# Two-block transformer kernel on one core: decay products at half width, decay subtractions on POOL, lower bounds computed once, dense groups in another order

## The chip, the core and the metric

The kernel runs on one core of a Trainium2 chip. It is written instruction by instruction: each engine (PE, DVE, ACT, POOL, and SP, which issues the DMAs) has its own list, and the engines meet only at semaphores that the program names. The metric is the device time of one execution in microseconds. Before the change the median of three runs is 3160.41 us (3159.9 to 3169.08).

## The reference, cut to what matters

Two blocks of two layers each work on 512 tokens of width 1024. The change is in the first block alone. Each of its layers projects the normed input and feeds three mixers: an mLSTM, an HGRN2, and a sliding-window attention with sinks. What bears on the change is the HGRN2 and its gate:

```
lb_all = jnp.cumsum(jax.nn.softmax(hgrn_lb_logits, axis=0), axis=0)
lb_all = lb_all - lb_all[0:1]                      # one lower bound per layer and column
...
log_f = jnp.logaddexp(jnp.log(lb), jnp.log1p(-lb) + jax.nn.log_sigmoid(fp))
key = (1.0 - lb) * jax.nn.sigmoid(-fp)
G = jnp.cumsum(log_f)                              # running sum over time
A[l, s] = sum_d q[l, d] * exp(G[l, d] - G[s, d]) * k[s, d]      for s <= l
o = A @ v
```

After the mixers each layer has the output projection, an MLP and an embedding gate:

```
x = x + concat([m_out, h_out, s_out]) @ w_out[l]
```

## The kernel before, in words

`part_one` loads tables, sums the squares of the input for the first norm, and then runs `layer_one` twice in a hardware loop. `layer_one` has one block of instructions for the projections and the mixers, then the MLP and the gate.

A product with float32 accuracy is made of three passes over operands that are split into a high and a low part. Weights come in panels of up to 1 MB: SP loads one into one of two raw buffers, ACT rounds it to the high part (`pan.high`), DVE subtracts to get the low part (`pan.low`), and PE uses both. In `layer_one` a "dense group" is one output bank of such a projection: 24 matmuls. Groups 0 to 3 are feature-major for the HGRN2's forget gate and query, 4 to 7 its values, 8 to 11 the mLSTM's convolution input, 12 its gates, then six token-major sets of four: mLSTM values, the window attention's keys and values and its two query halves, the mLSTM output gate `mo` and the HGRN2 output gate `hg`. A feature-major group has 512 moving columns per matmul, a token-major one 256. At the end stand the halves `first` and `second` of the output projection.

The HGRN2 is done in levels. For level `lv` with B = 2^(lv-1), each stretch of 2B tokens has its middle as reference; `G` is subtracted on both sides of it (`prepare`), exponentiated (ACT, `decay`), multiplied with keys and queries (DVE, `decay`), and multiplied out on PE (`products`). Levels 1 to 7 stay within a tile of 128 tokens: of each product only the part in which queries lie in the later half of a stretch is kept, through a predicated copy with a mask (`keep`). Levels 8 and 9 cross tiles and are copied by ACT (`keep_apart`). There are two column groups `c`, so 20 steps `k` of this loop, of which two are level 0. `W` has three slots, so a level can be prepared when the products of three levels earlier are done.

The order of work is written by hand. `dense_h`, `dense_m` and `dense_w` say at which step of the level loop, of the 16 mLSTM blocks (`block_scores`, `block_weights`, `block_exp`, `block_probs`) and of the 19 window steps (`scores`, `softmax`, `turn`, `result`) a dense group stands; all three engines walk the same tables. `released` makes PE wait until a group's bank has been emptied. `chunk_w` says when a chunk of the mixers' output is transposed for the output projection. The layer's lower bounds of the forget gate (`bounds`) are made in every layer between its norm and its first group.

## Time and profile before

| | us |
|---|---|
| median of three runs | 3160.41 |
| the profiled execution, its own time | 3157.43 |
| its span, first to last instruction | 3155.6 |
| PE busy | 2879.8 (91%) |
| DVE busy | 1667.7 (53%) |
| ACT busy | 1106.7 (35%) |
| POOL busy | 108.0 (3%) |

Busy shares are shares of the span. PE's matmuls overlap in the records, so a busy PE is not a PE at its peak; the granted clock beside it tells at which rate it ran. The mixers of the first layer lie between 42.5 and 374.6 us of the span, those of the second between 867.3 and about 1200 us, with the same shape. A stretch of the profile is read by three things: how long PE is idle in it, which engine's instruction ends that idle time, and the granted clock.

### The profile page before, as it was taken

The page shows a single profiled execution, that of the slowest core. Times are in us where ns is not written, and L with a number is a line of the kernel's source. Part 1 is how long each engine was busy: PE and PEld are TensorE (multiplying, and loading weights), DVE is VectorE, ACT ScalarE, POOL GpSimd, SP SyncE. Part 2 cuts the span into 40 slices and gives each one's busy share as a digit, 9 for nine tenths or more (in the row PEclk, how much of TensorE's full clock was granted, in tenths as well). Part 3 has the DMA queues.
Part 4 walks back from the last instruction along what each step waited for, and adds up shares of the span by engine and source line. Part 5 has one row for each costly group of instructions (what it writes and reads, how often), then busy time and mean ns, then how long its engine had stood idle before and what let it go on. Part 6 is the DMA issues. An engine that isn't in the chain of part 4 may idle for free. (4 is left out here: it accounts for less than half of the span.)

```text
span 3155.6 us, 37966 instructions
## 1 busy us (share of the span) xinstructions
PE 2879.8 (91%) x14756; PEld 2346.2 (74%) x14756; DVE 1667.7 (53%) x3011; ACT 1106.7 (35%) x1691; POOL 108.0 (3%) x88
## 2 busy tenths in 40 slices
PE   4798999999787989999996998899998998999998
PEld 3676778887666867888875887788886786778886
DVE  3656575555657555656655544553444544454442
ACT  4334332223453343222243444332332344332231
POOL 1000000000200000000020000000000000000000
PEclk9988899999888978999998999999998999999999
DMA  3110144443121102444422210132322210122322
GB/s 133 64 44 27 47 143 158 160 160 140 60 81 45 54 27 75 166 160 173 153 80 95 81 40 28 54 107 75 110 77 94 81 53 19 64 81 82 112 77 77
DMA packets 42993, 280.86 MB, mean 89 GB/s; under 512 B 5944, under 2 KB 6200, under 8 KB 11704
## 3 DMA queue, kind: packets, MB, share of 16 engines
q1 hardware_dynamic: 42808, 278.34, 25.4%
q8 instruction: 122, 2.00, 0.2%
q14 instruction: 63, 0.52, 0.1%
HBM read 276.23 MB, written 2.10 MB: 88 GB/s over the span
## 5 line engine op out<-in xcount | busy, mean ns | idle before, releaser
L303 DVE TENSOR_TENSOR low_panels<-raw_panels,high_panels 128x2048 fp32r<-128x2048 f32 (+3 forms) x218 | 469.2, 2153 | 345.1 <-ACT high_panels L291 345.0
L291 ACT ACTIVATE high_panels<-raw_panels 128x2048 fp32r<-128x2048 f32 (+3 forms) x218 | 392.5, 1801 | 494.9 <-PE bank L1419 150.6
L420 PE MATMUL bank<-mlp_h_high,high_panels 128*128 128x512 f32 x1152 | 457.3, 397 | 0.0
L420 PE MATMUL bank<-mlp_h_low,high_panels 128*128 128x512 f32 x1152 | 455.2, 395 | 0.0
L420 PE MATMUL bank<-mlp_h_high,low_panels 128*128 128x512 f32 x1152 | 455.1, 395 | 0.0
L420 PEld LDWEIGHTS bank<-mlp_h_high,low_panels 128*128 128x128 f32 x1152 | 216.1, 188 | 52.6
L420 PEld LDWEIGHTS bank<-mlp_h_low,high_panels 128*128 128x128 f32 x1152 | 216.2, 188 | 51.5
L420 PEld LDWEIGHTS bank<-mlp_h_high,high_panels 128*128 128x128 f32 x1152 | 216.2, 188 | 51.5
L445 PE MATMUL bank<-high_panels,h_high 128*128 128x256 f32 x704 | 211.6, 301 | 13.3 <-DVE arena L1100 12.7
L420 PE MATMUL bank<-h_high,high_panels 128*128 128x512 f32 x496 | 207.7, 419 | 12.9 <-DVE arena L1080 12.8
L1419 PE MATMUL bank<-mlp_hid_high,high_panels 128*128 128x512 f32 x512 | 204.5, 399 | 0.0
L445 PE MATMUL bank<-low_panels,h_high 128*128 128x256 f32 x704 | 202.4, 287 | 0.0
L1419 PE MATMUL bank<-mlp_hid_low,high_panels 128*128 128x512 f32 x512 | 202.4, 395 | 0.0
L1419 PE MATMUL bank<-mlp_hid_high,low_panels 128*128 128x512 f32 x512 | 202.3, 395 | 0.0
L445 PE MATMUL bank<-high_panels,h_low 128*128 128x256 f32 x704 | 201.6, 286 | 0.0
L420 PE MATMUL bank<-h_low,high_panels 128*128 128x512 f32 x496 | 199.1, 401 | 0.0
L420 PE MATMUL bank<-h_high,low_panels 128*128 128x512 f32 x496 | 198.4, 400 | 0.0
L1480 DVE SCALAR_TENSOR_TENSOR mlp_mod_acc<-raw_panels,conditioning,mlp_mod_acc 128x256 f32<-128x256 f32 x336 | 165.1, 491 | 12.0
L445 PEld LDWEIGHTS bank<-high_panels,h_high 128*128 128x128 f32 x704 | 138.2, 196 | 34.9 <-issue 19.8
L1963 ACT ACTIVATE masked_scores<-masked_scores,stats 128x128 f32<-128x128 f32 (+3 forms) x160 | 81.3, 555 | 216.7 <-DVE stats L2067 216.7
L445 PEld LDWEIGHTS bank<-low_panels,h_high 128*128 128x128 f32 x704 | 138.5, 197 | 1.5 <-issue 1.4
L2190 PE MATMUL bank<-mlp_hid_high,high_panels 128*128 128x512 f32 x352 | 139.0, 395 | 0.0
(344 smaller groups left out, 4900.5 us busy)
## 6 DMA issues: line engine op xcount, KB each, us to landing
raw_panels<-in_w SPq DMA_DIRECT2D x238, 1024.0 KB, 4.9
raw_panels<-in_w SPq DMA_DIRECT2D x16, 384.0 KB, 3.2
raw_panels<-in_w SPq DMA_DIRECT2D x4, 960.0 KB, 4.6
raw_panels<-in_w SPq DMA_DIRECT2D x4, 768.0 KB, 4.2
row<-in_row SPq DMA_DIRECT2D x2, 1220.0 KB
x<-in_xT SPq DMA_DIRECT2D x1, 2048.0 KB, 7.6
raw_panels<-in_w SPq DMA_DIRECT2D x4, 512.0 KB, 3.5
mix<-in_rope SPq DMA_DIRECT2D x2, 1024.0 KB, 7.7
```

What stands on the lines that cost most here:

```text
L291: self.nc.scalar.activation(self.g.high[:, i % SPLIT, 0:raw.shape[1]], raw, ACT.Copy).then_inc(self.high_ready, 1)
L303: self.nc.vector.tensor_tensor(self.g.low[:, i % SPLIT, 0:w], raw, self.g.high[:, i % SPLIT, 0:w].bitcast(F32), ALU.subtract).then_inc(sel ...
L420: ins = nc.tensor.matmul(bank[:, :], w[a][:, k, c0:c0 + P], rhs[b][:, k0 + k, :], start=first and k == 0 and j == 0, stop=last and k == kt ...
L445: ins = nc.tensor.matmul(bank[:, 0:n], rhs[b][:, k, t * P:(t + 1) * P], w[a][:, k, :], start=k == 0 and j == 0, stop=k == DC - 1 and j == 2)
L1419: ins = nc.tensor.matmul(b[:, :], w[a_][:, k, (m % 2) * P:(m % 2 + 1) * P], (uh, ul)[b_][:, k, :], start=k == 0 and j == 0, stop=k == DC - ...
L1480: ins = nc.vector.scalar_tensor_tensor(o, w[:, k, :], g.cond[:, k:k + 1], o, ALU.mult, ALU.add)
L1963: nc.scalar.activation(o, o, ACT.Exp, bias=g.negmax[:, 2 * i + m:2 * i + m + 1], scale=u.scale).then_inc(w.probs_ready, 1)
L2190: ins = nc.tensor.matmul(b[:, :], w[a_][:, k, (c % 2) * P:(c % 2 + 1) * P], (uh, ul)[b_][:, k0 + k, :], start=part == 0 and k == 0 and q = ...
```

## The change

1. The opening block of the program is merged into `part_one`'s. The input `x` is loaded first and in two halves, the sum of its squares starts after the first half, and tables, the rope angles, the first panel and the lower bounds of both layers (`bounds`) are made in the same block. A layer copies its bounds from there.
2. The first eight dense groups go to eight different banks instead of two, so none of them waits for a bank.
3. The subtractions of `prepare` move from DVE to POOL. ACT and DVE make the decays of step k+1 (ACT: k+2) during step k instead of those of step k.
4. Products of levels 1 to 7 are made for the later halves only, 64 columns per matmul instead of 128. Levels 1 to 5 are kept by DVE with masks of half width; levels 6 and 7 are copied by ACT block by block (`MASKED = 5`).
5. Dense groups: the panel of `mo` is loaded earlier, and its four groups stand in the level loop, which now holds 13 groups instead of 9. The 16 mLSTM blocks hold the 12 window groups instead of 20, the four groups of `hg` stand at the first four window steps. In a step, PE takes the dense group ahead of the scores.
6. The gates' sigmoid (`mo`), the silu of the convolution and the exponential `em` stand on ACT at step 17; the silu of `hg` at window step 4. The mLSTM weights are made a block ahead; the transposes of the window's queries start before the last two blocks and rotate over three banks.

```diff
+MASKED = 5
-    out += [k("w_in", c) for c in (C_MVO, C_SKV, C_SQ, C_SQ + PW, C_MVO + PW, C_HIG + PW)]
+    out += [k("w_in", c) for c in (C_MVO, C_MVO + PW, C_SKV, C_SQ, C_SQ + PW, C_HIG + PW)]
...
             def _(sp):
+                sp.dma_start(g.x[:, 0:DC // 2, :], a["xT"][:, 0:DC // 2, :]).then_inc(s("x_begun"), 16)
+                sp.dma_start(g.x[:, DC // 2:DC, :], a["xT"][:, DC // 2:DC, :]).then_inc(s("x_loaded"), 16)
+                sp.dma_start(kc[:, :], a["kc"]).then_inc(s("start_loaded"), 16)
...
-        dense_h = {1: [8], 3: [9], 5: [10], 7: [11], 9: [12], 11: [13], 13: [14], 15: [15], 17: [16]}
+        dense_h = {2 * i: [n_before + i] for i in range(5)}
+        dense_h.update({10 + i: [n_before + 5 + i] for i in range(8)})
         dense_m = {}
-        for i, j in enumerate(range(17, 37)):
-            dense_m.setdefault(2 * i // 3 if i < 12 else i - 4, []).append(j)
-        dense_w = {i: [first_groups[c]] for c, i in enumerate((7, 8, 9, 10, 12, 13, 16, 17))}
-        chunk_w = {2: [2], 3: [3], 5: [0], 6: [1], 7: [4], 11: [5], 15: [6], 18: [7]}
+        for i, j in enumerate(window_groups):
+            dense_m.setdefault(3 * i // 4, []).append(j)
+        dense_w = {i: [hg_groups[i]] for i in range(NT)}
+        dense_w.update({i: [first_groups[c]] for c, i in enumerate((8, 9, 10, 12, 13, 14, 16, 17))})
+        chunk_w = {4: [0], 5: [1], 6: [2], 7: [3], 8: [4], 11: [5], 15: [6], 18: [7]}
...
         def dense_bank(i):
-            return bank[1 + i % 2]
+            return bank[(3, 4, 1, 2, 5, 6, 0, 7)[i]] if i < n_before else bank[1 + i % 2]
...
             def _(pool):
                 nc.gpsimd.memset(vaug[:, :, :, MD:MD + 1], 1.0).then_inc(s("ones_ready"), 1)
+                pool.wait_ge(s("g_summed"), 2)
+                def prepare(k):
...
+                    if j >= 3:
+                        kk = j - 3 + (j - 3) // len(LEVELS) + 1
+                        pool.wait_ge(s("d_products"), 2 * kk + 2)
...
+                    nc.gpsimd.tensor_tensor(out[:, :, 0:B], ref, blk[:, :, 0:B], ALU.subtract)
+                    nc.gpsimd.tensor_tensor(out[:, :, B:2 * B], blk[:, :, B:2 * B], ref, ALU.subtract).then_inc(s("d_span"), 1)
...
+                            if within:
+                                B = LEVELS[lv - 1]
+                                q = q.rearrange("p (b w) -> p b w", w=2 * B)[:, :, B:2 * B]
+                                to = to.rearrange("p (b w) -> p b w", w=B)
...
-                    products(k)
                     if k == NL + 1:
                         results(0)
-                    if k == 18:
+                    products(k)
+                    if k == 15:
                         turn_gates()
+                    if k == 17:
+                        spread(0)
...
+                        if lv <= TILE_LEVELS:
+                            B = LEVELS[lv - 1]
+                            for o in range(0, P, 2 * B):
+                                ins = nc.scalar.activation(AT[o:o + B, m, :].rearrange("p (t w) -> p t w", t=NT)[:, :, o + B:o + 2 * B],
+                                                           b[o:o + B, 0:2 * P].rearrange("p (t w) -> p t w", t=NT)[:, :, o // 2:o // 2 + B], ACT.Copy)
...
+                decay(1)
                 for k in range(n_levels):
-                    decay(k)
+                    if k + 2 < n_levels:
+                        decay(k + 2)
                     if k >= 1:
                         keep_apart(k - 1)
                     for i in dense_h.get(k, []):
                         evict(i)
-                    if k == 11:
+                    if k == 10:
                         gate_logs()
-                    if k == 13:
+                    if k == 17:
                         conv_open()
+                        act.wait_ge(kept_v, by_dve[at_panel[8]])
+                        nc.scalar.activation(mo, mo, ACT.Sigmoid).then_inc(s("mo_open"), 1)
+                        act.wait_ge(s("gates_by_token"), 1)
+                        nc.scalar.activation(em, cm[:, 16:32], ACT.Exp, scale=-1.0).then_inc(s("em_ready"), 1)
...
-                    if p == 0:
+                    if p == 4:
                         act.wait_ge(kept_v, by_dve[at_panel[12]])
-                        nc.scalar.activation(mo, mo, ACT.Sigmoid).then_inc(s("gates_open"), 1)
-                        nc.scalar.activation(hg, hg, ACT.Silu).then_inc(s("gates_open"), 1)
+                        nc.scalar.activation(hg, hg, ACT.Silu).then_inc(s("hg_open"), 1)
...
                 for k in range(n_levels):
                     if k + 1 < n_levels:
-                        prepare(k + 1)
-                    decay(k)
+                        decay(k + 1)
                     if k >= 1:
                         keep(k - 1)
...
-                    if 9 <= k < 9 + CONV1:
-                        conv(k - 9)
+                    if 9 <= k < 9 + 2 * CONV1:
+                        conv((k - 9) % CONV1, (0, 2) if k < 9 + CONV1 else (1, 3))
```

The order of instructions, place one: POOL's list in a layer, from the memset that opens it. Before, the additions of the next norm's squares follow at once:

```order
L644 MEMSET arena 128x16
L346 TENSOR_TENSOR norm_buffers<-norm_buffers 128x512
L349 TENSOR_TENSOR norm_buffers<-norm_buffers 128x512 x5
```

After, 36 subtractions stand between them, of which these are the first eight (`arena` holds `G` and `W`):

```order
L692 MEMSET arena 128x16
L707 TENSOR_TENSOR arena<-arena 128x256
L708 TENSOR_TENSOR arena<-arena 128x256
L707 TENSOR_TENSOR arena<-arena 128x128x2
L708 TENSOR_TENSOR arena<-arena 128x128x2
L707 TENSOR_TENSOR arena<-arena 128x64x4
L708 TENSOR_TENSOR arena<-arena 128x64x4
L707 TENSOR_TENSOR arena<-arena 128x32x8
L708 TENSOR_TENSOR arena<-arena 128x32x8
```

Each pair is one level; its shape splits the 256 columns into ever fewer and longer runs.

Place two: DVE in the middle of the level loop, levels 4 and 5 of the first column group. L1136 and L1137 are `prepare`, L1147 and L1148 `decay`, L1162 the masks of `keep`:

```order
L1136 TENSOR_TENSOR arena<-arena 128x16x16
L1137 TENSOR_TENSOR arena<-arena 128x16x16
L1147 TENSOR_TENSOR arena<-arena 128x32x8
L1148 TENSOR_TENSOR arena<-arena 128x32x8
L1162 COPY_PREDICATED arena<-k,bank 128x512 x2
L1136 TENSOR_TENSOR arena<-arena 128x8x32
L1137 TENSOR_TENSOR arena<-arena 128x8x32
```

The same place after; L1211 and L1212 are now `decay`, L1234 the masks:

```order
L1211 TENSOR_TENSOR arena<-arena 128x32x8
L1212 TENSOR_TENSOR arena<-arena 128x32x8
L1234 COPY_PREDICATED arena<-k,bank 128x128x2 x2
L1211 TENSOR_TENSOR arena<-arena 128x16x16
L1212 TENSOR_TENSOR arena<-arena 128x16x16
L1234 COPY_PREDICATED arena<-k,bank 128x64x4 x2
```

A level has four DVE instructions instead of six, and the two masks have 256 columns instead of 512.

Place three: ACT at the end of the level loop. Before (L925 is the decays' exponential, L951 the convolution's silu, L937 and L939 `keep_apart`, L1020 `em`, L957 the first mLSTM block):

```order
L951 ACT_TABLE_LOAD
L951 ACTIVATE norm_buffers<-norm_buffers 128x512 x4
L925 ACT_TABLE_LOAD
L925 ACTIVATE arena<-arena 128x512 x6
L937 ACTIVATE arena<-bank 128x2x128 x2
L939 ACTIVATE arena<-bank 128x512 x2
L1020 ACTIVATE small<-small 128x16
L957 ACTIVATE arena<-arena,small 128x512
```

After (L1033 the silu, L1102 the sigmoid of `mo`, L1104 `em`, L1016, L1019 and L1021 `keep_apart` of levels 7, 8 and 9, L1039 the first block):

```order
L1000 ACTIVATE arena<-arena 128x512 x3
L1016 ACTIVATE arena<-bank 32x4x32 x4
L1033 ACT_TABLE_LOAD
L1033 ACTIVATE norm_buffers<-norm_buffers 128x512 x4
L1102 ACT_TABLE_LOAD
L1102 ACTIVATE arena<-arena 128x1024
L1104 ACT_TABLE_LOAD
L1104 ACTIVATE small<-small 128x16
L1016 ACTIVATE arena<-bank 64x4x64 x2
L1019 ACTIVATE arena<-bank 128x2x128 x2
L1039 ACTIVATE arena<-arena,small 128x512
L1021 ACTIVATE arena<-bank 128x512 x2
```

The copies of levels 7 to 9 stand behind the silu, the sigmoid and `em` with their three table loads; the exponentials of all levels stand ahead of them.

## Rows read from the trace of the kernel before

**Rows 1.** Stretches: window us, its length, busy us of each engine, PEclk, DMA

```profile
0.00:34.00 34.00, 3.57 (x16) 3.49 (x16) 4.24 (x22) 6.72 (x12) 7.92 (x11) 1.00 0.35 131
56.50:96.00 39.50, 27.41 (x147) 24.29 (x146) 16.73 (x21) 24.93 (x25) 0.00 (x0) 0.78 0.21 67
96.00:190.20 94.20, 74.95 (x556) 62.27 (x555) 69.60 (x138) 33.79 (x48) 0.00 (x0) 0.90 0.13 45
190.20:241.70 51.50, 51.29 (x368) 45.78 (x367) 20.30 (x41) 18.63 (x83) 0.00 (x0) 0.95 0.18 62
241.70:288.80 47.10, 42.94 (x321) 35.97 (x320) 29.93 (x74) 15.41 (x28) 0.00 (x0) 1.00 0.13 45
288.80:323.00 34.20, 25.11 (x115) 18.52 (x116) 22.73 (x84) 20.52 (x45) 0.00 (x0) 0.60 0.00 1
323.00:374.60 51.60, 45.67 (x247) 36.03 (x246) 27.46 (x107) 18.83 (x52) 0.00 (x0) 0.90 0.12 42
867.30:1224.30 357.00, 304.89 (x1889) 251.68 (x1889) 208.44 (x492) 148.18 (x300) 7.76 (x6) 0.88 0.15 52
```

**Rows 2.** PE's waits, second layer's mixers: who, for whom, us in total, times, longest

```profile
PE bank L695 <- DVE arena L1148: 19.5, 11, 8.0
PE bank L809 <- ACT arena L987: 11.4, 8, 5.0
PE bank L420 <- DVE arena L1080: 6.4, 1, 6.4
PE bank L445 <- DVE arena L1100: 6.3, 3, 5.7
```

**Rows 3.** PE's timeline (start us, us): a token-major group, a feature-major one, `results`

```profile
93.07 0.28 PE L445 MATMUL bank<-high_panels,h_high 128*128 128x256 f32 x1
...
95.97 1.16 PE L695 MATMUL bank<-arena 64*128 64x128 f32 x16
97.06 0.50 PE L420 MATMUL bank<-h_high,high_panels 128*128 128x512 f32 x1
...
102.86 1.16 PE L695 MATMUL bank<-arena 64*128 64x128 f32 x16
...
145.72 4.68 PE L712 MATMUL bank<-arena 128*128 128x64 f32 x40
```

**Rows 4.** Start, timeline: start, us; last row, DMA: KB, us to landing

```profile
13.12 6.90 POOL L349 TENSOR_TENSOR norm_buffers<-norm_buffers 128x512 f32<-128x512 f32 x5 [0.74 <-ACT norm_buffers L337]
...
33.16 0.26 ACT L508 ACTIVATE cos_sin<-norm_buffers 128x64 f32<-128x64 f32 x1 [13.89 <-DVE norm_buffers L503]
...
33.92 0.36 SPq L634 DMA_DIRECT2D vec<-in_vec  x1
...
x<-in_xT SPq DMA_DIRECT2D x1, 2048.0 KB, 7.6
```

**Rows 5.** ACT's timeline where the bounds are made, first layer

```profile
54.60 1.28 ACT L874 ACT_TABLE_LOAD   x1 [1.17 <-DVE lower_bounds L1064]
```

**Rows 6.** DVE by line in the level loop: count, busy us, mean ns, idle before

```profile
L1162 DVE COPY_PREDICATED arena<-k,bank 128x512 f32<-128x512 int32 x32 | 21.4, 720 | 5.9 <-issue 5.9
L1180 DVE SCALAR_TENSOR_TENSOR norm_buffers<-arena,vec,norm_buffers 128x512 f32<-128x512 f32 x12 | 8.2, 741 | 0.0
...
L1148 DVE TENSOR_TENSOR arena<-arena 128x256 f32<-128x256 f32 x18 | 7.4, 414 | 0.0
L1136 DVE TENSOR_TENSOR arena<-arena 128x256 f32<-128x256 f32 x18 | 7.4, 411 | 0.0
L303 DVE TENSOR_TENSOR low_panels<-raw_panels,high_panels 128x2048 fp32r<-128x2048 f32 x3 | 6.8, 2279 | 1.4 <-ACT high_panels L291 1.4
```

**Rows 7.** ACT's timeline at the first window step: the sigmoid of `mo`

```profile
292.41 1.06 ACT L1042 ACTIVATE arena<-arena 128x1024 f32<-128x1024 f32 x1
```

**Rows 8.** POOL and DVE side by side in the embedding gate, timeline

```profile
830.32 1.29 POOL L349 TENSOR_TENSOR norm_buffers<-norm_buffers 128x512 f32<-128x512 f32 x1 [2.81 <-ACT norm_buffers L337]
830.34 1.82 DVE L1612 TENSOR_TENSOR ple_gate<-ple_gate,ple_emb 128x512 f32<-128x512 f32 x1
```

More of the change, by code:

```diff
@@ new lines, in _ @@
+                st.link(nc.vector.tensor_tensor(parts[:, 2, :], parts[:, 1, :], parts[:, 0, :], ALU.subtract))
+                for i in range(DEPTH):
+                    st(nc.vector.tensor_scalar(bounds[:, i, 1, :], parts[:, 1, :], lsel[:, i, 0:1], lsel[:, i, 1:2], ALU.mult, ALU.add))
+                    st.link(nc.vector.tensor_scalar(bounds[:, i, 2, :], parts[:, 2, :], lsel[:, i, 0:1], None, ALU.mult))
+                    nc.vector.tensor_tensor(bounds[:, i, 0, :], bounds[:, i, 2, :], bounds[:, i, 1, :], ALU.subtract).then_inc(s("bound_ready"), 1)
@@ L510, in part_one, with layer_one @@
+                act.wait_ge(s("bound_ready"), DEPTH)
+                for i in range(DEPTH):
+                    nc.scalar.activation(bounds[:, i, 3, :], bounds[:, i, 2, :], ACT.Exp)
         with nc.Fori(0, DEPTH) as l:
-            layer_one(nc, g, a, s, pan, l, k1, vec, row, gb, cs, lb, lsel, small)
-def layer_one(nc, g, a, s, pan, l, k1, vec, row, gb, cs, lb, lsel, small):
+            layer_one(nc, g, a, s, pan, l, k1, vec, row, gb, cs, bounds, lb, small)
+def layer_one(nc, g, a, s, pan, l, k1, vec, row, gb, cs, bounds, lb, small):
@@ L559, in layer_one @@
         turns = region(6664, 320)
-        gap, rest = small[:, 216:218], small[:, 218:220]
+        gap, floor, gain, rest = (lb[:, i, :] for i in range(4))
         sinks = small[:, 300:300 + QH]
@@ L620, in level_kept @@
         def level_kept(eng, k):
-            within = levels[k][1] <= TILE_LEVELS
-            n = 2 * sum((lv <= TILE_LEVELS) == within for _, lv in levels[:k + 1])
+            within = levels[k][1] <= MASKED
+            n = 2 * sum((lv <= MASKED) == within for _, lv in levels[:k + 1])
             eng.wait_ge(d_kept if within else ao_kept, n)
@@ L861, in _ @@
                         turn_chunk(c)
-                    for i in dense_w.get(p, []):
-                        dense(i)
                 for i in second_groups:
@@ L905, in forget_logs @@
                 def forget_logs():
-                    st.link(nc.scalar.activation(rest, lb[:, 2, :], ACT.Exp))
                     act.wait_ge(s("f_opened"), 2)
@@ L2294, in program @@
             s = Semaphores(nc, sems)
[L2295 to L2318 removed]
+            part_one(nc, g, a, s, kc)
         with ExitStack() as sems:
```

300 lines of the change are left out of this document (159 added, 141 removed).

## The prediction, made before the changed kernel ran

> **What bounds the kernel now.** I read the busy table first: PE 91%, DVE 53%, ACT 35%, POOL 3%. PE is the engine whose list decides, but the mean hides two kinds of loss, idle time and time at the lower clock. So I cut the first layer's mixers into stretches and looked at PE's idle time and clock in each [rows 1]. From 56.5 to 96 PE is busy 27.4 of 39.5 us, in the level loop (96 to 190.2) 75 of 94.2, in the first half of the mLSTM blocks 51.3 of 51.5, in the window steps 70.8 of 85.8, at a granted clock of 0.60 in their first 34 us. Then I asked what ends the waits [rows 2]: 19.5 us in 11 waits for DVE's decay products, 6.4 and 5.7 us in one wait each for a bank that DVE has to empty, and 11.4 us for ACT at the window steps, 5.0 of it at once. The second layer's mixers take as long as the first's, so what a layer gains counts twice. The MLPs and the second block are not touched.
>
> Sizes of the units, at the full clock: a token-major dense group is the way from 93.07 to 95.97, 2.9 us; a feature-major one from 97.06 to 102.86, 5.8 us; `results` 4.7 us; the products of a level about 1.1 us [rows 3]. At half clock they are nearly twice that.
>
> **Start.** Before, the squares run on ACT and POOL (five additions take 6.90 us, so 1.4 a chunk), PE sums, the block ends, and only then do tables load and DVE make the angles; the sine at 33.16 is last, and the layer's first load goes out at 33.92 [rows 4]. Now `x` goes first. Its 2048 KB took 7.6 us behind `kc`; its first half should be there some 4 us before the 9.8 us at which the squares began. POOL ends the additions at about 16 instead of 20, ACT its squares at 15. Behind them ACT has a silu, exp and ln with a table load each (1.28 us [rows 5], so 3 x 1.5 = 4.5), then sine (1.5) and the exponentials of the bounds (1.7): 23, instead of 33.4. DVE's angles lie beside that. Gain 10.5 us; each layer pays 0.35 for two small instructions ahead of its norm. Bounds 7 (the many loads arrive late) and 12.
>
> The Trainium skill (ScalarE: Activation LUTs, What ACT_TABLE_LOAD costs) puts a table load at about 2.7 us. Our trace has 1.28 for it, so I use 1.28; by the page the start would gain 7 us less, and the removed loads in the layers would be worth more.
>
> **Groups 0 to 7 (56.5 to 96).** This takes 39.5 us for two feature-major and four token-major groups, which are 2 x 5.8 + 4 x 2.9 = 23.2 us of work [rows 1, 3]. The rest is the two waits of 6.4 and 5.7 and PE at half clock behind them. Both waits are for banks: group 2 waits until ACT, which first makes the bounds with table loads in front [rows 5], and DVE have emptied bank 1; group 5 or 6 waits for DVE, which stands behind a panel. With eight banks and no bounds neither is left. Gain 16 us. What is late next: the running sum `G`. ACT is busy 24.9 us in this stretch [rows 1], some 4 of it for the bounds and their share of the table loads; the other 21, without PE's waits between, end at about 77. Behind that DVE has a low panel of 2.3 [rows 6] and two scans, done at 82, POOL its first two subtractions, 84, then exponential and product, 85.5. PE now has dense group 8 first and wants the products of level 1 at about 87. It fits by 1 to 2 us. Bounds 10 (it slips, and the clock falls) and 17.
>
> **Level loop.** Before, a pair of steps is one group of 5.8, two products and a wait of 1.0, 9.05 us; later the waits are 8.0, 3.4 and a few of 0.8. DVE has 69.6 us of work in 94.2 [rows 1]. Of that go the 36 subtractions (2 x 7.4) and of the 32 masks of 0.72 eight altogether (5.8), while twenty become half as wide (20 x 0.31 = 6.2) [rows 6]; a two-input instruction of 256 columns at 0.41 is my price for such a mask. DVE is left with 43 us, and the moved `mo` groups bring four evictions of 0.4 and a panel of 2.3: 47. For PE the half-wide products save at most 0.2 us a level; I take nothing. In the first half (five feature-major groups) PE is alone the bound: 5 x 5.8 + 10 x 1.1 = 40 us, from 80 to 120. In the second there are eight groups of 2.9, ten products, `results` 4.7 and small things, 23.2 + 11 + 4.7 + 1 = 40 us on PE, but about 30 of DVE's 47 us lie here, since the convolution (12 x 0.74 [rows 6] and four more) and the gates stand here, and DVE waits some 5 us for `results` in the middle. Either holds the other up for a step: I put the end of the last dense group at 160. Then ACT: the silu (2048 columns), the sigmoid (1024, 1.06 us [rows 7]) and `em`, with three table loads of 1.28, are 2.3 + 1.1 + 0.2 + 3.8 = 7.4 us in front of the copy of level 7, and PE's last product waits for that copy. The blocks begin at 170, 90 us behind group 7, against 94.2 before, with 11.6 us more dense work in it. Gain 4 us. Bounds: 100 us (every DVE product is late) and 82 (DVE hidden).
>
> **POOL's price.** No row shows a subtraction of 256 columns in short runs. The nearest is 1.29 us for 512 columns in a piece [rows 8]; half of that is 0.65, and on DVE the short runs cost nothing, all 18 of L1136 average 0.41 [rows 6]. I take 0.7; bounds 0.41, DVE's own, and 1.3, the full-width row. At 1.3 a level takes 2.6 us of POOL, still under the 4.1 us of a PE step, and there are three slots: hidden at either bound.
>
> **Blocks (190.2 to 288.8, 98.6 us).** Twelve token-major groups now stand in blocks 0 to 8, before in 0 to 7: 51.5 us, PE-bound with no wait [rows 1]; the same. The rest loses eight groups, 23.2 of 42.9 us of PE, and is then DVE's, which is busy 29.9 us there [rows 1]; eight evictions of 0.41 and two panels of 2.3 [rows 6] leave 22, and I take 23. Transposes and the last block result add 6, and the first `hg` group 3. Sum 83.5, gain 15. Bounds 8 (the products' half clock, because PE is thin there) and 20.
>
> **Window steps (85.8 us).** The 5.0 us wait goes: it was sigmoid and silu of 1.06 with three table loads [rows 2, 5, 7], 6.0 in all. Three more `hg` groups come in at a clock of 0.60 [rows 1], where I price them 3.5 instead of 2.9 or 5.1: +10.5. The silu at step 4 with two table loads costs ACT 3.6, of which I let 2 show. Loss 6. Bounds: loss 14 (half clock throughout, silu in full), gain 1 (they fall into idle time).
>
> **Sum.** A layer: 16 + 4 + 15 - 6 = 29; two layers 58; start 10.5 less 0.7: 68 us. From the profiled execution, 3157.4 - 68 = 3089.5. The median of the runs lies 3.0 above that execution, so I forecast 3093 us, 2.1% less.
>
> **Rivals.** (a) *POOL holds DVE up.* In [rows 8] a DVE instruction with two SBUF inputs starts with a POOL one and lasts 1.82 us; others of 128x512 take 0.74 [rows 6]. So it waited for POOL to end, while in the level loop POOL is free before. There 36 POOL instructions of 0.7, 25 us, now meet decays, convolution and panels. In the first half DVE has room. In the second 18 of them, up to 12.6 us, fall on the engine that already decides; with the other slips a layer gains 17 instead of 29: 3117. For it: the row. Against: products of the mLSTM and evictions read PSUM, and POOL's work is a third of the time. The Trainium skill states this as a lock (SBUF — State Buffer, SBUF: two separate sides): whichever of the two starts first has the pair for its whole instruction. By that rule each collision costs the rest of one instruction, which is this rival; the trace agrees.
> (b) *PE stays at full clock.* With no long wait left before the window steps, they and the `hg` groups run at 2.4 GHz: 9 us more a layer, 3074. Against: the later blocks are thin.
> (c) *POOL paces the levels, and it is slower than before.* Its 36 subtractions are a chain with the products; short runs may cost more on it than on DVE. At t each, the blocks begin at 82 + 36t + 4 where I have 170. Two layers lose their 29 and the start's 10 when that is 34 later, so at t = 3.3 us; at 4 us the time is 3212. For it: no row. Against: 1.29 for twice the columns.
> (d) *The time comes back.* Same engines, moved waits: thin blocks at half clock, each `hg` group 5.1, levels at 100. A layer gains 4: 3142.
>
> **Chances.** Forecast 0.62 (its own range 3075 to 3110), (a) 0.18, (b) 0.11, (c) 0.04, (d) 0.05. Range 3068 to 3125: it takes in (a) and (b) and leaves out (c), (d) and the tails. A difference under 0.3% (9 us) can't be told from none. Faster 0.94; same 0.02; slower 0.04, which is (c).
>
> **What would show it.** In the trace after: the first layer's load of `vec` at 23 to 24 us; no wait of PE between groups 1 and 7; POOL pairs of 1.4 us, and DVE decays near 0.42, longer if (a) holds; last dense group of the level loop some 104 us behind the end of group 1, then a wait of 4 to 6 us for ACT; blocks in 80 to 88 us with DVE busy at their end; window steps of 88 to 96 us. I am wrong if POOL instructions last over 2 us, if PE waits for DVE more than 15 us a layer in the level loop, or if the clock in the window steps stays at 0.6 with `hg` groups in them.

## The result, and the profile of the changed kernel

The changed kernel takes 3143.1 us in the median of four runs (3140.2 to 3144.8), the kernel before 3161.5 beside it: ratio 0.9941, 95% interval 0.9921 to 0.996. It is faster by 18 us, where the prediction had 68 (3093, range 3068 to 3125).

First the stretches of the first layer again, as in [rows 1]: window, its length, then busy time of PE, PEld, DVE, ACT and POOL, the granted clock, the DMA share and GB/s.

```profile
32.30:68.90 36.60, 36.57 (x193) 31.19 (x194) 22.39 (x26) 29.15 (x29) 0.00 (x0) 1.00 0.29 101
68.90:105.40 36.50, 36.50 (x250) 29.36 (x249) 23.75 (x40) 14.38 (x22) 12.69 (x20) 1.00 0.25 87
105.40:162.10 56.70, 45.52 (x404) 41.68 (x403) 40.72 (x68) 26.43 (x40) 14.83 (x16) 0.89 0.17 57
162.10:224.00 61.90, 56.66 (x372) 49.53 (x371) 19.32 (x41) 20.06 (x86) 0.00 (x0) 0.90 0.15 52
224.00:260.40 36.40, 29.31 (x150) 22.73 (x149) 21.61 (x61) 10.65 (x24) 0.00 (x0) 0.62 0.00 1
260.40:290.00 29.60, 22.96 (x154) 18.41 (x154) 20.00 (x72) 16.87 (x37) 0.00 (x0) 0.89 0.11 36
290.00:359.30 69.30, 56.54 (x281) 44.01 (x281) 34.30 (x124) 21.90 (x60) 0.00 (x0) 0.80 0.09 31
```

The first row is the dense groups 0 to 7, the next two the level loop, the fourth blocks 0 to 8, the fifth the late blocks (9 to 15) with the transposes and the first `hg` group, the last two the window steps. PE is full at clock 1.00 until 105, and then never again: each later stretch has idle time, a clock under 1, or both. Then PE's waits from 68.9 to 359.3 (who, for whom, us in total, times, longest):

```profile
PE bank L446 <- DVE arena L1179: 6.3, 3, 3.1
...
PE bank L773 <- ACT arena L1016: 6.1, 1, 6.1
PE bank L819 <- DVE arena L1287: 5.6, 2, 3.4
PE bank L799 <- DVE arena L1271: 4.1, 1, 4.1
...
PE bank L421 <- DVE h_low L1368: 2.8, 1, 2.8
```

The waits of [rows 2] for DVE are gone: of 19.5 us for the decays none is left. But waits of 3 to 6 us in all have taken their place, all on other instructions: a dense bank that DVE has not emptied (L1179), the copy of level 7 (L1016), the last operation of the gates (L1271), the low half of a chunk (L1368). The same by stage, first layer:

| stage | before | after | gain | predicted |
|---|---|---|---|---|
| start, to the first dense matmul | 42.5 | 32.3 | 10.2 | 10.5, less 0.35 |
| groups 0 to 7 | 53.5 | 36.6 | 16.9 | 16 |
| level loop | 94.2 | 93.2 | 1.0 | 4 |
| blocks | 98.6 | 98.3 | 0.3 | 15 |
| window steps and second groups, to the MLP's norm | 114.0 | 127.1 | -13.1 | -6 |

The last line as windows, before and after:

```profile
288.80:402.80 114.00, 95.90 (x472) 74.31 (x472) 61.46 (x202) 50.12 (x110) 7.77 (x6) 0.84 0.11 38
```

```profile
260.40:387.50 127.10, 104.60 (x546) 82.11 (x545) 65.02 (x207) 49.55 (x109) 7.75 (x6) 0.86 0.12 42
```

A layer gains 5 us, not 29. The second layer repeats the first: it gains 6 (from its first dense matmul to its MLP's norm). The second layer's MLP norm, whose first matmul (L376, in the kernel before L375) is the mark that I use for all runs below, starts 22.2 us earlier:

```profile
1228.81 0.92 PE L375 MATMUL bank<-kc,norm_by_token 128*128 128x128 f32 x4 [2.08 <-DVE norm_by_token L367]
```

```profile
1206.62 1.22 PE L376 MATMUL bank<-kc,norm_by_token 128*128 128x128 f32 x4 [2.08 <-DVE norm_by_token L368]
```

All that follows the mark is the same 8994 matmuls in both kernels, and it is not equally long in the two profiled executions (windows of before, then of after):

```profile
1228.80:3155.60 1926.80, 1820.79 (x8994) 1477.96 (x8994) 954.84 (x1610) 649.11 (x903) 57.88 (x45) 0.97 0.26 90
```

```profile
1206.60:3143.00 1936.40, 1826.29 (x8994) 1483.11 (x8994) 955.09 (x1610) 649.26 (x903) 57.90 (x45) 0.97 0.26 89
```

DVE's and ACT's busy times agree within 0.3 us; PE is busy 5.5 us longer with the same matmuls and idles 4 us more. So 22.2 us of gain become 12.6 between these two spans, and 18 between the medians. I therefore give the mark beside the median. The mark is free of what follows it, but it comes from one execution: that of the changed kernel was the slowest of its four runs, those of e1, e2, e3 and c2 the fastest of theirs. A difference of a few us at the mark is shown only where the medians, whose runs don't overlap, or both layers say the same.

### The profile page after: what moved, and what is told of

It is laid out like the page before. It is cut to its first block and busy times, and to the rows that moved or that the text cites. A ratio compares the mean times of both kernels' runs of the same rounds, so it can differ in the third digit from the quotient of the medians.

```text
span 3143.0 us, 37948 instructions
## 1 busy us (share of the span) xinstructions
PE 2890.2 (92%) x14756; PEld 2357.6 (75%) x14756; DVE 1637.5 (52%) x2921; ACT 1113.8 (35%) x1712; POOL 163.0 (5%) x160
## 5 line engine op out<-in xcount | busy, mean ns | idle before, releaser
L421 PE MATMUL bank<-h_high,high_panels 128*128 128x512 f32 x496 | 208.6, 421 | 10.1 <-DVE h_low L1368 5.6
L1492 PE MATMUL bank<-mlp_hid_high,high_panels 128*128 128x512 f32 x512 | 204.3, 399 | 0.0
L347 POOL TENSOR_TENSOR norm_buffers<-norm_buffers 128x512 f32<-128x512 f32 x11 | 16.3, 1479 | 2506.2 <-ACT norm_buffers L338 2506.2
```

Of the source, the lines that this page charges most:

```text
L347: nc.gpsimd.tensor_tensor(total, g.sq[:, 0, :], g.sq[:, 1, :], ALU.add).then_inc(e.sum_used, 2)
L421: ins = nc.tensor.matmul(bank[:, :], w[a][:, k, c0:c0 + P], rhs[b][:, k0 + k, :], start=first and k == 0 and j == 0, stop=last and k == kt ...
L1492: ins = nc.tensor.matmul(b[:, :], w[a_][:, k, (m % 2) * P:(m % 2 + 1) * P], (uh, ul)[b_][:, k, :], start=k == 0 and j == 0, stop=k == DC - ...
```

## The experiments

The edits e and u are made to the changed kernel, each alone. Mark: start of the second layer's MLP norm.

| run | mark, us | median (lowest to highest), us | ratio to before, 95% |
|---|---|---|---|
| changed kernel | 1206.6 | 3143.1 (3140 to 3145) | 0.9941, 0.9921 to 0.9960 |
| e1_evict_first | 1190.0 | 3124.2 (3123 to 3128) | 0.9883, 0.9866 to 0.9901 |
| e2_act_late | 1202.8 | 3137.8 (3130 to 3143) | 0.9927, 0.9909 to 0.9945 |
| e3_hg_in_blocks | 1200.1 | 3138.2 (3130 to 3144) | 0.9930, 0.9908 to 0.9952 |
| e4_gates_later | 1198.6 | 3136.8 (3134 to 3139) | 0.9919, 0.9901 to 0.9936 |
| u1_two_banks | 1226.9 | 3166.9 (3161 to 3172) | 1.0015, 1.0004 to 1.0025 |
| u2_dve_subtract | 1209.9 | 3145.2 (3144 to 3147) | 0.9945, 0.9928 to 0.9961 |
| u3_full_width | 1207.8 | 3140.9 (3137 to 3146) | 0.9933, 0.9917 to 0.9950 |
| u4_probs_behind | 1194.2 | 3126.1 (3124 to 3132) | 0.9884, 0.9864 to 0.9903 |
| w1_windows_only | 1192.2 | 3130.8 (3127 to 3135) | 0.9906, 0.9891 to 0.9922 |
| c1_four_edits | 1174.1 | 3107.5 (3101 to 3109) | 0.9817, 0.9800 to 0.9835 |
| c2_chunks_earlier | 1151.1 | 3097.9 (3085 to 3107) | 0.9804, 0.9778 to 0.9829 |
| c3_groups_earlier | 1184.8 | 3117.0 (3099 to 3119) | 0.9836, 0.9804 to 0.9869 |
| c4_gather_first | 1173.2 | 3099.4 (3094 to 3108) | 0.9793, 0.9777 to 0.9810 |
| c5_probs_behind | 1156.6 | 3087.3 (3085 to 3094) | 0.9769, 0.9756 to 0.9782 |

### The order in the blocks: e1 and u4

`block_probs` is the product of the exponentials with PE's scores (L1287). In the blocks PE's own order is the same before and after: the dense group stands ahead of the scores. What the change moved is DVE's list, and ACT's exponentials with it.

```diff
-                    block_probs(j)
-                    ...
                     for i in dense_m.get(j, []):
                         evict(i)
+                    block_probs(j)
+                    ...
```

> From the changed kernel, in the mLSTM blocks DVE empties a block's dense banks before it multiplies the block's scores (L1287), not after. Theory 'the eviction is queued behind the scores': DVE waits 15 us and less at a time for PE's scores in blocks 0 to 8, and PE's waits of 3.08 and 0.83 us for L1179 and the groups of 5.5 us at half clock behind them come from that. The waits go, the block stage falls from 98.3 to about 92 us a layer, the kernel from 3143 to about 3131. Rival 'PE is thin and DVE has its work anyway': the wait moves to the scores, which DVE now multiplies later; under 2 us a layer, 3140 to 3144.

What DVE does in the changed kernel around PE's wait of 3.08 us, which ends at 195.1 (timeline: start us, us):

```profile
192.16 0.29 DVE L1287 SCALAR_TENSOR_TENSOR arena<-bank,arena 128x128 f32<-128x128 f32 x1 [4.87 <-PE bank L819]
192.37 2.28 DVE L304 TENSOR_TENSOR low_panels<-raw_panels,high_panels 128x2048 fp32r<-128x2048 f32 x1
194.57 0.75 DVE L1179 TENSOR_TENSOR arena<-bank,row 128x256 f32<-128x256 f32 x2
```

DVE stands idle 4.87 us at the product L1287, because PE makes the scores (L819) behind the two dense groups of the same step; the panel and both evictions stand behind it. PE then has two full banks and nothing to do. The same place in e1:

```profile
189.99 2.29 DVE L304 TENSOR_TENSOR low_panels<-raw_panels,high_panels 128x2048 fp32r<-128x2048 f32 x1 [3.08 <-ACT high_panels L292]
192.20 0.75 DVE L1179 TENSOR_TENSOR arena<-bank,row 128x256 f32<-128x256 f32 x2
```

The product now stands behind both; the panel starts 2.4 us earlier and DVE no longer waits 4.9 us for the scores. Its waits for them in the first nine blocks (before: where the eight dense blocks are), in the order before, changed kernel, e1, u4:

```profile
DVE arena L1214 <- PE bank L741: 0.4, 2, 0.2
```

```profile
DVE arena L1287 <- PE bank L819: 48.4, 8, 15.4
```

```profile
DVE arena L1287 <- PE bank L819: 3.4, 7, 0.7
```

```profile
DVE arena L1285 <- PE bank L819: 0.8, 4, 0.2
```

These are waits by their releaser and not DVE's idle time as a whole, which went from 31 to 43 us: in e1 DVE idles for panels and banks instead. What counts is which instructions stand behind the wait. The mark comes 16.6 us earlier (6.6 in the first layer, 10.0 in the second), the median falls by 19: the theory, and more than it asked for. u4 puts the order of before back on DVE and ACT:

```diff
-                block_weights(0)
-                for j in range(n_blocks):
-                    if j + 1 < n_blocks:
-                        block_weights(j + 1)
-                    block_probs(j)
+                for j in range(n_blocks + 1):
+                    if j < n_blocks:
+                        block_weights(j)
+                    if j >= 1:
+                        block_probs(j - 1)
```

> From the changed kernel, the mLSTM blocks have the order of before on DVE and ACT: the weights of block j, then the products of block j-1 with its scores, then the dense evictions. Theory 'the new order holds the evictions behind PE's scores': DVE no longer waits for the scores of its own step, the waits of 3.08 and 0.83 us for L1179 go, the first nine blocks are back at some 54 us from 61: 3143 to about 3130. Rival 'the late blocks need the order a step ahead': the blocks behind the last dense group grow by as much, since each score then waits for a product one step later, and 3140 to 3150 results.

12.4 us at the mark and 17 in the median. In the medians, undoing this one part is worth nearly as much again as the whole change had brought (18). The same matmuls, from the scores of block 0 to those of block 8, in the changed kernel, e1 and u4:

```profile
168.70:223.10 54.40, 49.16 (x322) 42.61 (x321) 19.32 (x41) 15.77 (x75) 0.00 (x0) 0.91 0.17 59
168.70:216.90 48.20, 46.19 (x321) 40.04 (x320) 17.47 (x37) 16.04 (x77) 0.00 (x0) 0.96 0.20 66
169.20:213.80 44.60, 44.60 (x321) 38.52 (x320) 17.57 (x37) 16.71 (x82) 0.00 (x0) 1.00 0.21 72
```

In u4 PE has no idle time there and the full clock. The rival has a part: from there to the first window scores u4 takes 39.4 us where the changed kernel took 37.3, and has 7.3 us of waits for the products where that had 5.6.

### Two waits in the level loop: e2 and e4

```diff
-                    if k == 17:
+                    if k == 19:
                         conv_open()
                         ... (sigmoid of mo, exponential em)
```

> From the changed kernel, ACT's silu of the convolution, sigmoid of mo and exponential em (three table loads) stand behind the copies of levels 6, 7 and 8 of the second pair of heads instead of ahead of the last three of them. Theory 'one engine's queue': PE's wait of 6.09 us for L1016 goes, and the product behind it runs at full clock; the two dense groups ahead of the first scores cover the silu. 6 us a layer, so 3143 to about 3131. Rival 'the same work waits somewhere else': the first scores wait for the silu instead, 0 to 2 us a layer, 3139 to 3143.

ACT's queue in the changed kernel, with three table loads between the copies of level 6 and of level 7 (both L1016):

```profile
150.76 1.10 ACT L1016 ACTIVATE arena<-bank 32x128 f32<-32x128 f32 x4
151.88 1.28 ACT L1033 ACT_TABLE_LOAD   x1
...
159.04 0.22 ACT L1104 ACTIVATE small<-small 128x16 f32<-128x16 f32 x1
159.28 0.65 ACT L1016 ACTIVATE arena<-bank 64x256 f32<-64x256 f32 x2
```

In e2 the wait of 6.1 is gone and the first scores come 8.4 and 7.8 us earlier, but from there the blocks take 5 to 8 us longer, with a 2.0 us gap of PE ahead of `results` and it and a group at half clock. At the mark 3.8 remain, all of it from the first layer, in the median 5.3 with runs (3130 to 3143) that overlap those of the changed kernel: nearer the rival. In this kernel the evictions still queue behind the scores, and the time won here runs into the next wait; c1 below has both edits.

```diff
-                    if k == 15:
+                    if k == 16:
                         turn_gates()
-                    if k == 17:
+                    if k == 18:
                         spread(0)
...
-                    if k == 16:
+                    if k == 17:
                         gates(4)
```

> From the changed kernel, the transposes of the gates stand one step later in the level loop (16 instead of 15), with DVE's copy and the first spread a step later too. Theory 'a wait of one instruction': PE's wait of 4.09 us for L1271 goes, and with it the half-clock group of 5.1 us behind it: 5 to 6 us a layer, 3143 to about 3132. Rival 'DVE is behind in the whole second half of the level loop' (31 us busy of 35.7): PE waits for decays or masks instead, 0 to 2 us a layer, 3139 to 3143.

PE's waits of e4 in the level loop:

```profile
PE bank L773 <- ACT arena L1016: 5.4, 1, 5.4
PE bank L446 <- DVE arena L1179: 1.4, 1, 1.4
```

The wait for the gates is gone, 1.4 us of it is back at a bank. It brings 8.0 us for two layers at the mark and 6.3 in the median: between the theory (10 to 12) and the rival (0 to 4).

### The window steps: e3 and w1

```diff
-        dense_w = {i: [hg_groups[i]] for i in range(NT)}
+        dense_m.update({9 + i: [hg_groups[i]] for i in range(NT)})
+        dense_w = {}
```

> From the changed kernel, the four hg groups stand in blocks 9 to 12 instead of window steps 0 to 3. Theory 'a dense group belongs where PE idles': blocks 9 to 15 take 33.4 us at a clock of 0.59 with PE busy 26.3; with four groups more they take at most 4 us longer at a higher clock, while the window steps fall from 98.9 to about 87. Gain 8 us a layer, 3143 to about 3127. Rival 'a group costs 3 us wherever it stands': the blocks grow by 10 to 12 us and the clock of the window steps falls back to 0.6; 3140 to 3148.

The window steps to the MLP's norm fall from 127.1 to 121.0 us in both layers, the blocks grow by 2 to 3.4. The four groups cost 6 us in the window steps, where the expectation had 12, and 2 to 3 in the blocks: half of the theory at the mark (6.5), and 4.9 in the median, with runs (3130 to 3144) that overlap those of the changed kernel. More edits follow in w1: chunks at steps 3 to 7 instead of 4 to 8, the two of the HGRN2 first, and the silu of `hg` in a block.

```diff
-        chunk_w = {4: [0], 5: [1], 6: [2], 7: [3], 8: [4], ...}
+        chunk_w = {3: [2], 4: [3], 5: [0], 6: [1], 7: [4], ...}
```

> From the changed kernel, only what e3 and c2 have: hg groups in blocks 9 to 12, silu of hg in block 13 of ACT, chunks turned at steps 3 to 7. Theory 'the window steps lost 6 us to the hg groups and 6 to chunks and silu': scores of window 0 to the end of the mixers falls from 127 to 117 us a layer while the blocks grow by at most 3, so 3143 to about 3128, 8 to 10 below e3's 3138. Rival 'the clock in this stretch is by chance, and c2 had luck': 121 to 124 us a layer, 3135 to 3138.

Windows of e3, then of w1, from the first window scores to the norm:

```profile
263.30:384.30 121.00, 98.89 (x472) 75.81 (x472) 61.63 (x202) 47.69 (x108) 7.75 (x6) 0.80 0.10 36
```

```profile
263.00:379.90 116.90, 95.89 (x473) 74.05 (x473) 61.74 (x202) 44.21 (x105) 7.77 (x6) 0.83 0.10 37
```

116.9 in both layers, as the theory had it, and 3130.8 in the median. By these profiles, of the 13 us that the window steps lost, 6 were the groups and 4 the place of chunks and silu. The last 3 stay open. The 4 are less sure than the 6: with the early chunks of w1 the same stretch took 116.4 us in c2 and 123.6 and 120.1 in c4, and 122.7 in c1 with the late ones, so the rival isn't excluded.

### The parts of the change by themselves: u1, u2, u3

```diff
-            return bank[(3, 4, 1, 2, 5, 6, 0, 7)[i]] if i < n_before else bank[1 + i % 2]
+            return bank[1 + i % 2]
... (and the first eight groups wait for their bank again)
```

> From the changed kernel, the dense groups 0 to 7 alternate between two banks again; the bounds stay made once. Theory 'the banks carry the 17 us of groups 0 to 7': PE waits again for ACT and DVE to empty a bank, 10 us a layer or more, and the time goes from 3143 to about 3163. Rival 'the running sum G sets the level loop anyway': PE waits there, but the level loop ends as before, and 3143 to 3150 results.

PE's waits of u1 in the first layer's groups 0 to 7:

```profile
PE bank L446 <- DVE arena L1175: 5.6, 1, 5.6
...
PE bank L421 <- DVE arena L1155: 2.9, 1, 2.9
```

Both bank waits of [rows 2] are back, the second with 2.9 us instead of 6.4, the first products come 11.7 and 10.1 us later, the level loop takes no longer than in the changed kernel (92.6 us), and the gain of the whole change is gone: 3167 against 3164 for the kernel before beside it. The banks carry 20 us, and nothing behind them hides it.

u2 puts `prepare` back on DVE: step k+2 is prepared during step k, a step ahead of DVE's own decay products.

```diff
-                    nc.gpsimd.tensor_tensor(out[:, :, 0:B], ref, blk[:, :, 0:B], ALU.subtract)
+                    nc.vector.tensor_tensor(out[:, :, 0:B], ref, blk[:, :, 0:B], ALU.subtract)
... (the second subtraction likewise)
```

> From the changed kernel, the 36 decay subtractions of a layer are made by DVE again (0.41 us each, 14.8 us), and decays no longer meet POOL. Theory 'POOL's collisions cost little next to what it takes off DVE': DVE, busy 31 of 35.7 us in the second half of the level loop, gets 7.4 us more there and gives back about 5 us of stretched instructions; PE waits 3 to 6 us more a layer, 3143 to about 3151. Rival 'POOL holds DVE up': the decays fall from 0.55 and 0.51 to 0.41 us, the convolution from 0.82 to 0.74, and the level loop is as fast or faster; 3135 to 3143.

DVE and POOL in the level loop of the changed kernel, then DVE in u2 (count, busy us, mean ns):

```profile
L708 POOL TENSOR_TENSOR arena<-arena 128x256 f32<-128x256 f32 x18 | 15.2, 842 | 0.0
L707 POOL TENSOR_TENSOR arena<-arena 128x256 f32<-128x256 f32 x18 | 13.3, 741 | 99.2 <-PE bank L773 50.9 <-DVE arena L1199 48.3
L1211 DVE TENSOR_TENSOR arena<-arena 128x256 f32<-128x256 f32 x18 | 10.0, 555 | 7.2 <-ACT arena L1000 7.1
L1251 DVE SCALAR_TENSOR_TENSOR norm_buffers<-arena,vec,norm_buffers 128x512 f32<-128x512 f32 x12 | 9.3, 816 | 0.0
L1212 DVE TENSOR_TENSOR arena<-arena 128x256 f32<-128x256 f32 x18 | 9.2, 509 | 0.0
```

```profile
L1247 DVE SCALAR_TENSOR_TENSOR norm_buffers<-arena,vec,norm_buffers 128x512 f32<-128x512 f32 x12 | 8.4, 743 | 0.0
L1207 DVE TENSOR_TENSOR arena<-arena 128x256 f32<-128x256 f32 x18 | 7.5, 419 | 0.1
L1208 DVE TENSOR_TENSOR arena<-arena 128x256 f32<-128x256 f32 x18 | 7.5, 418 | 0.0
```

Decays and convolution take 28.5 us beside POOL and 23.4 without: POOL stretches them by 5 us a layer and takes 15 off. The mark moves by 3.3 us, the median by 2: less than this comparison can tell from nothing. The move of the subtractions to POOL is worth nothing that could be seen, and costs nothing either.

In u3 PE multiplies 128 columns again where the changed kernel has 64; only the used half is kept.

```diff
-                        n = P // 2 if within else (t1 - t0) * P
+                        n = (t1 - t0) * P
... (and the masks and copies read the later halves out of the full width)
```

> From the changed kernel, PE's products of levels 1 to 7 are full width again (128 columns a tile instead of 64); the masks and the copies still take only the half that is used. Theory 'the half width is worth next to nothing to PE' (a pair of levels in the first half takes 2.0 us at PE where before had 2.3): 28 levels and both layers at 0.1 to 0.2 us, 3143 to about 3147. Rival 'the half width keeps the masks off the banks sooner and so shortens DVE's path': PE's waits of 0.86 and 4.08 us grow by 2 us, 3150 or more.

1.2 us later at the mark, 2 us less in the median: no difference, as the theory had it. The masks of half width, which u3 keeps, were not tested by themselves.

### Together: c1 to c5

c1 has e1, e2, e3 and e4.

> The changed kernel with four edits at once: evictions ahead of the products in the blocks, ACT's silu, sigmoid and em behind the copies of levels 6 to 8, the hg groups in blocks 9 to 12, and the gates' transposes a step later. Alone they took 16.6, 4, 7 and 8 us off the two layers' mixers by their profiles. Theory 'the waits are apart from each other': the sum, 35 us, 3143 to about 3108. Rival 'they share one slack' (the first scores wait for the silu, whatever stands ahead): only e1's and e3's part stays, 3118 to 3122.

3107.5, 35.6 us less in the median and 32.5 at the mark, where the four alone make 16.6 + 3.8 + 6.5 + 8.0 = 34.9 (in the medians 18.9 + 5.3 + 4.9 + 6.3 = 35.4). So e2's part, which alone was lost in the blocks, is no longer lost: the waits are nearly apart from each other.

c2 is c1 with the chunks and the silu of w1. c3 and c4 are c2 with one edit each:

```diff
-        ... enumerate((8, 9, 10, 12, 13, 14, 16, 17))
+        ... enumerate((7, 8, 9, 10, 12, 13, 16, 17))
```

```diff
+                    if j == 1:
+                        gather(1)
                     for i in dense_m.get(j, []):
                         evict(i)
                     block_probs(j)
-                    if j == 1:
-                        gather(1)
```

> The four edits of c1, and in the window steps the chunks of the mixers' results turned at steps 3 to 7 instead of 4 to 8 (the hg half first), with the silu of hg in block 13 of ACT. Theory 'a wait ends at half clock': PE's wait of 2.78 us for chunk 3's low half goes, and with it the half-clock group of 5.5 us behind it, and ACT's two table loads leave the window steps: 4 to 6 us a layer, 3107 to about 3097. Rival 'PE idles between window steps whatever stands there': the wait moves into the steps before, at most 1 us a layer, 3105 to 3108.

> c2, and the eight first groups at window steps 7, 8, 9, 10, 12, 13, 16, 17, as before the change, instead of 8, 9, 10, 12, 13, 14, 16, 17. Theory 'the groups one step later cost the gap at the steps without one': the first nine steps keep PE busier, another 2 to 3 us a layer below c2. Rival 'the first group then waits for chunk 1 in the same way as it did in the changed kernel for chunk 3': the wait of 2.8 us and the half-clock group come back, c2 plus 5 to 10 us.

> c2, and in block 1 DVE gathers the second pair's results (L1239 of c1) before it evicts and multiplies, not after. Theory: PE's wait of 1.32 us for the gather at the spread of the second head goes, 1 to 1.5 us a layer, c2 less 2 to 3 us. Rival: PE then waits for the eviction behind it, no change against c2.

c2 gives 3097.9, as expected, but its runs lie 22 us apart, and c4 can't be told from it. c3 is 19 us slower in the median (three runs at 3117 to 3119, one at 3099), more than its rival had. It has the wait of 2.8 us for L1369 back, and its window steps take 124.5 us in both layers against 116.4 in c2. That is 16 of the 34 us at the mark, but c4 took 120.1 and 123.6 for the same stretch with c2's order, so how much of it is the edit's stays open. The other 18 lie in levels and blocks, which are the same code in c2 and c3. The windows of c2, then c3, from the scores of block 0 to those of block 8, and then the second layer of c1, whose first layer took what c2 took:

```profile
157.10:205.40 48.30, 44.94 (x322) 38.59 (x321) 20.08 (x41) 20.16 (x84) 0.00 (x0) 1.00 0.19 66
```

```profile
158.30:213.80 55.50, 52.73 (x322) 45.71 (x321) 20.08 (x41) 20.24 (x85) 0.00 (x0) 0.85 0.17 58
```

```profile
957.20:1011.00 53.80, 51.02 (x322) 44.66 (x321) 20.08 (x41) 20.20 (x84) 0.00 (x0) 0.87 0.18 60
```

and `results` behind the same gap of PE, in c2, in c3, and in the second layer of c1:

```profile
158.95 4.65 PE L791 MATMUL bank<-arena 128*128 128x64 f32 x40 [0.77 <-issue]
```

```profile
160.22 7.84 PE L791 MATMUL bank<-arena 128*128 128x64 f32 x40 [0.76 <-issue]
```

```profile
959.08 7.25 PE L791 MATMUL bank<-arena 128*128 128x64 f32 x40 [0.77 <-issue]
```

c5 is c2 with the order of u4 in the blocks.

> c2, but with the order of before in the blocks on DVE and ACT (weights of block j, products of block j-1, then the evictions) instead of the order a step ahead with the evictions first. Theory 'either order that lets the evictions through is as good': block stage 84 to 86 us, 3098 within 5. Rival 'a step ahead is what the late blocks need': the late blocks take 5 us more, 3104 to 3110.

It has the lowest median, 3087.3 us, with five runs (3085 to 3094), below both expectations. But it isn't shown to be faster than c2: the fastest run of each is 3085.3, their intervals meet, and c2's mark is 5.5 us earlier. From the first scores to the window scores c5 takes 88.1 us in both layers against 85.7 in c2, outside the 84 to 86 that were expected. From the end of the level loop on, first layer:

```profile
152.30:224.00 71.70, 70.64 (x500) 60.22 (x498) 36.94 (x81) 34.00 (x110) 0.00 (x0) 1.00 0.16 60
224.00:246.30 22.30, 18.24 (x96) 15.89 (x94) 9.13 (x28) 8.62 (x13) 0.00 (x0) 0.54 0.00 0
246.30:290.00 43.70, 35.85 (x156) 26.97 (x156) 26.62 (x102) 18.67 (x52) 0.00 (x0) 0.61 0.00 1
```

PE idles 1.1 us of the 71.7 in the first row, which holds the blocks' dense groups, at the full clock. What is left is the low clock behind the last dense group, 224 to 290.

## Why the prediction was wrong

**Start: right.** The layer's first load goes out at 23.51 us (predicted 23 to 24), and the gain is 10.2 with table loads of 1.28 as in [rows 5]. By the Trainium skill (ScalarE: Activation LUTs, What ACT_TABLE_LOAD costs) a switch of tables costs 2.66 us, of which the load is 1283 ns and a drain about 1380 ns. The trace agrees on the load and shows no drain: between 15.30 and 22.69 us ACT's five loads take 1.28 each, the instruction behind each starts 1.29 or 1.30 us after its load, and the next load follows that instruction within 0.03 us. With five drains the start would, by an estimate from the Trainium skill's figure, have gained 7 us less.

**Groups 0 to 7: right.** 16.9 where I had 16. u1 shows that the banks carry 10 to 12 of it; that the rest is the bounds, now made once, was not tested by itself.

**Level loop: too much by 3.** The wait of 4 to 6 us for ACT was foreseen and came as 6.1. The one of 4.1 for the gates was not: I counted 30 us of DVE work against 40 of PE and left it at that, while PE stands at one instruction (L799) whose chain on DVE ends late. e4 shows 4 us a layer for it at the mark. My sum of DVE's work was also too low, 47 us where 64.5 were measured: the masks gave back 9.0 us and not 12.0 (the half-wide ones last 0.55 us each, where I priced 0.41), POOL's collisions stretch DVE's work, and DVE's two scans for `G` fall into this window now. That miss lies mostly in the first half of the loop, where PE was busy all the time, and cost nothing there.

**Blocks: the step that failed.** I wrote that the twelve groups in blocks 0 to 8 would take "51.5 us, PE-bound with no wait; the same". They took 61.9, and the late blocks 36.4 where I had 32: 10.4 and 4.4 of the 15 us that are missing. The change moves `block_probs(j)` from one step behind to its own step, ahead of the evictions; the prediction gives that no price. DVE's waits for PE's scores in the first nine blocks went from 0.4 us in the kernel before to 48.4, PE waited 3.1 and 0.8 us for full banks behind them, and a group ran at half clock. e1 and u4 each undo that in another way: from the scores of block 0 to those of block 8 the changed kernel takes 54.4 us, e1 48.3 and u4 44.6, in both layers. So the order carries 6 to 10 of the 10.4 us. The 4.4 of the late blocks are not explained by it (u4 takes 2 us more there). In the changed kernel and in c5 these blocks run at a low clock, 0.62 and 0.54, and the changed kernel waits 5.6 us for single products in them. I had priced them by busy times, 23 us of DVE work; that a chain of steps that wait for each other needs more is what I take from it, but no run tests it.

**Window steps: the direction right, the size not.** -13.1 for -6, near the outer bound of -14. The groups are not the cause of the missing 7 us (e3: 6 where I had 10.5). By its profile w1 shows 4 for chunks and silu, which I had priced 2 and had not seen as a wait of PE (2.8 us for L1368, then a group of 5.5 at half clock). The foreseen gain did come: PE's waits there for ACT fell from 11.4 us to 6.2 (L886). So counted against my own terms more than the last 3 us are open.

**Rival (a), POOL holds DVE up: the mechanism is there, its price is not.** Two-input instructions of 0.42 us take 0.51 to 0.56 in the mean beside POOL, 5 us a layer and not 12.6, and taking them away changed nothing that could be seen (u2). By the Trainium skill (SBUF — State Buffer, SBUF: two separate sides) a DVE instruction with two SBUF inputs and a POOL instruction that reads SBUF exclude each other for the whole instruction; the trace agrees, in that both get longer beside each other. POOL's own instruction was rightly priced (0.7; 0.74 and 0.84 measured), and (c) is out.

**Rival (d) gave 3142 and the measured time is 3143,** with a chance of 0.05. Thin stretches at half clock and gains that come back later as waits did happen. But the levels were not at 100, and the largest single cause, the order in the blocks, was in none of the cases. That its number fits is in good part luck.

**The signs.** None of the three signs of being wrong came: POOL's instructions last 0.79 us in the mean, PE waits 5 us for DVE in the level loop, the clock of the window steps is 0.89 and 0.80. What failed were two of the signs of being right: blocks of 98.3 us for 80 to 88, window steps of 98.9 for 88 to 96.

**And some 4 us of the miss may be no mechanism of the change.** By the mark the kernel gained 22.2, by the medians 18.4; in these two executions the untouched remainder was 9.6 us longer.

## What to carry to other kernels

When a change moves an instruction that waits past others in its queue, price what stands behind it: here one product moved ahead of the evictions on DVE cost 6 to 8 us a layer at the mark, more than POOL, the half-wide products or the placement of four groups. A wait of 3.1 us on PE cost about 5.5, since the group behind it took 5.4 us at half clock where such a group takes 2.9 at the full one; so look for the many small waits that a removed long one leaves behind, and take them out together: the four edits of c1 added up. Here the two stages without such waits (groups 0 to 7, the start) came within 1 us of a forecast from their units; the stages of short steps between engines, forecast from the engines' busy times, missed by 3, 15 and 7.

## What the runs showed of the hardware

The clock is not a function of the program. With the same instructions and a gap of 0.77 or 0.76 us ahead, `results` took 4.65 us in c2 (full clock, 2.4 GHz) and 7.84 in c3 (mostly at 1.2 GHz). In c1 it took 4.65 us in the first layer and 7.25 in the second, in one execution of one loop. From the scores of block 0 to those of block 8 the granted clock was 1.00 in c2 and 0.85 in c3, for 48.3 and 55.5 us. The run times of c2 spread by 22 us, those of c5, where that gap is 0.16 us, by 9; no run shows that the gap is the reason, and c1, with the gap of 0.77, spreads by 8.

Products of 64 columns are hardly faster than those of 128. The products of the level loop by shape, changed kernel, then u3 (where 48 of the 272 are 128 wide in both):

```profile
L773 PE MATMUL bank<-arena 64*128 64x64 f32 x224 | 14.8, 275 | 1.0 <-DVE arena L1234 0.9
```

```profile
L768 PE MATMUL bank<-arena 64*128 64x128 f32 x272 | 18.9, 282 | 1.0 <-DVE arena L1229 0.8
```

And POOL's subtractions of 256 columns, 0.74 and 0.84 us in the mean, take less where DVE stands idle beside them (one of them; the longest beside a busy DVE took 1.58):

```profile
98.84 0.61 POOL L707 TENSOR_TENSOR arena<-arena 128x256 f32<-128x256 f32 x1 [5.38 <-PE bank L773]
```

That is 0.61 us, against 0.42 on DVE.
